# A two-layer hybrid decoder trunk: VectorE sums the opening's squares, one norm product, norm means in PSUM, and a new order of the attention steps

## The reference

```python
for l in range(DEPTH):                                  # 2
    h = rmsnorm(x, attn_norm[l])
    proj = einsum('bsd,de->bse', h, w_in[l])            # 1024 -> 2304 columns
    sb_q, sb_k, sb_v, sw_q, sw_k, sw_v = split(proj)    # 3 x 8 heads; 8, 2 and 2 heads, of 64
    sb_o = stick_breaking_attention(sb_q, sb_k, sb_v)   # strictly causal, in blocks of 128 queries:
        # z = q k / 8;  a = exp(log_sigmoid(z) + suffix sum of -softplus(z));  o = a v
    sw_q, sw_k = rope(sw_q, positions), rope(sw_k, positions)
    sw_o = sliding_window_sink_attention(sw_q, sw_k, sw_v, sinks[l])     # window 128, softmax with a sink
    mix = concat(rmsnorm(sb_o, sb_norm[l]), rmsnorm(sw_o, swa_norm[l]))
    x = x + einsum('bse,ed->bsd', mix, w_out[l])
    h = rmsnorm(x, mlp_norm[l])
    x = x + einsum('bsf,fd->bsd', square(relu(einsum('bsd,df->bsf', h, w_up[l]))), w_down[l])
return rmsnorm(x, final_norm)
```

## Time and profile before

| | us |
|---|---|
| median of 3 executions | 1188.58 (1187.75 to 1190.56) |
| the profiled execution | 1187.64 |
| its span, first to last instruction | 1185.9 |
| TensorE busy | 1154.5 (97%) |
| VectorE busy | 554.3 (47%) |
| ScalarE busy | 589.4 (50%) |
| GpSimd busy | 574.3 (48%) |

### The profile page before, as it was taken

The page is one execution under the profiler, slowest core; times in us unless marked ns, Lnnn a source line. Parts: engine busy times, 40 slices in busy tenths (PEclk is TensorE's granted clock), DMA queues, the critical chain, the costliest instruction groups (busy, mean ns, idle before and its releaser), DMA issues.

```text
span 1185.9 us, 15498 instructions
## 1 busy us (share of the span) xinstructions
PE 1154.5 (97%) x5546; PEld 968.4 (82%) x5546; DVE 554.3 (47%) x785; ACT 589.4 (50%) x940; POOL 574.3 (48%) x310
## 2 busy tenths in 40 slices
PE   7999998999999999999999999899999999999996
PEld 5788887878888888888888889687888888888886
DVE  7766678765222222223355666758532222222224
ACT  5789898544133233133346888965431422322442
POOL 3454754664444444444754564456454444444452
PEclk9999999999999999999999999999999999999999
DMA  5220211223322323222222121012233232232222
GB/s 188 72 71 19 90 36 36 91 87 99 99 94 100 107 88 105 90 89 96 99 72 72 54 69 50 25 54 90 89 107 107 89 103 93 88 106 88 97 81 72
DMA packets 30027, 99.65 MB, mean 84 GB/s; under 512 B 3600, under 2 KB 5648, under 8 KB 29968
## 3 DMA queue, kind: packets, MB, share of 16 engines
q1 hardware_dynamic: 28992, 97.80, 25.1%
q10 hardware_dynamic: 976, 1.08, 0.3%
HBM read 96.77 MB, written 2.10 MB: 83 GB/s over the span
## 4 chain that ended last, share of the span: by engine, by line
PE 88%; ACT 4%; DVE 3%; issue 1%; DVEq 1%; ACTq 1%; DMA 1%; SPq 0%
PE DW L441 24%; PE DW L443 24%; PE DW L442 24%; PE Z L441 2%; PE Z L443 2%; PE Z L442 2%; PE Z L594 2%; PE DW L528 2%; PE O L607 1%; PE Z L577 1%; PE O L552 1%; PE DW L524 1%; ACTq L813 1%; DMA raw<-in_weights 1%; PE DW L538 1%
## 5 line engine op out<-in xcount | busy, mean ns | idle before, releaser
L951 POOL TENSOR_TENSOR w<-raw,w 128x1024 fp32r<-128x1024 f32 x178 | 429.8, 2416 | 409.4 <-ACT w L701 405.5
L701 ACT ACTIVATE w<-raw 128x1024 fp32r<-128x1024 f32 x177 | 185.8, 1051 | 224.0 <-PE DW L443 212.4
L441 PE MATMUL DW<-xm,w 128*128 128x512 f32 x512 | 200.3, 391 | 1.6 <-issue 1.6
L441 PE MATMUL DW<-stage,w 128*128 128x512 f32 x512 | 199.5, 390 | 0.6 <-DVE stage L1256 0.6
L442 PE MATMUL DW<-xm,w 128*128 128x512 f32 x512 | 199.3, 389 | 0.0
L443 PE MATMUL DW<-xm,w 128*128 128x512 f32 x512 | 199.3, 389 | 0.0
L443 PE MATMUL DW<-stage,w 128*128 128x512 f32 x512 | 199.3, 389 | 0.0
L442 PE MATMUL DW<-stage,w 128*128 128x512 f32 x512 | 199.3, 389 | 0.0
L1281 DVE TENSOR_TENSOR kf<-o 128x512 f32<-128x512 f32 x64 | 58.1, 908 | 195.7 <-ACT o L886 195.5
L1297 DVE TENSOR_TENSOR DW<-DW,probs 128x512 f32<-128x512 f32 x62 | 43.4, 699 | 224.1 <-PE DW L443 224.1
L441 PE MATMUL DW<-xa,w 128*128 128x512 f32 x296 | 119.6, 404 | 9.5 <-DVE xa L1064 7.5
...
## 6 DMA issues: line engine op xcount, KB each, us to landing
raw<-in_weights SPq DMA_DIRECT2D x179, 512.0 KB, 3.3
...
```

Of the source, the lines that this page charges most:

```text
L441: pe.matmul(bank, w[:, slot, 0, k], rhs[:, 0, c], start=start, stop=False)
L701: act.activation(w[:, slot_of(l * PACKS + p), 0], raw[:, p % 2], ACT.Identity).then_inc(w_hi, 1)
L951: pool.tensor_tensor(w[:, slot, 1], raw[:, p % 2], w[:, slot, 0].bitcast(F32), ALU.subtract).then_inc(w_ready, 1)
```

## The change

- In the opening VectorE adds all eight squares by seven adds, in a tree, and splits the third pack between them; both had been in part GpSimd's. It begins the angle after that. GpSimd waits for the sum before its first split. `NP` is gone, and `NA` in layer 0 is one product of the whole sum.
- The mean of the attention, stick-breaking and MLP norms goes to the PSUM bank W in place of SBUF, and the first two refining steps too; the bank is freed after the last. The sliding-window norm and the closing ones stay as they were.
- The last head's BD: ScalarE squares into the bank O, and VectorE adds that.
- `zl_full` counts the last head's scores apart from the other heads'.
- Both lists of steps are ordered anew; the tiles are the same.

```diff
-T0 U0 AG0 T1 CH3 U1 NP0 NA0 NAE0 NAD0 NAF0 TE0 T2 CL3 AG1 TH0 CH4 AG2 CL4 AG3 T3 U2 U3 AG4 AG5 TL0 CH5 TE2 AG6
-RE2 TE1 AG7 AG8 T4 AG9 CL5 TH1 AG10 AG11 TL1 SN0 U4 TE3 RS2 RM2 RA2 RE3 RS3 RM3 TH2 T5 U5 TL2 RA3 CH6 TE4 TH3
...
-T8 XE1 XH0 XL0 XH1 U8 BE2 WE1 WR1 CH10 WN1 CH11 T9 XL1 BP2 BS3 TE8 BH2 WT1 U9 TH8 SQ0 WH1 BL2 BX2 SA0 TL8 WL1
...
-BP10 WA6 XH9 WT7 WO6 WD6 TH16 BS11 T17 WH7 WL7 BE11 SQ5 TL16 SA4 WA7 BP11 XL9 CL19 BH10 CH20 SQ6 WO7 SA5 BL10
-WD7 U17 BH11 BL11 BX10 SQ7 GH0 XE10 BA4 TE17 GL0 SA6 SA7 NW0 XH10 BO4 BS12 NWE0 BD4 NWD0 NWF0 BE12 MN0 BX11
-MN1 XL10 XE11 BS13 BP12 XH11 BE13 MN2 BP13 BH12 XL11 MH0 VT17 BL12 BH13 VH17 BA5 MN3 MH1 MH2 ML0 ML1 BL13 BX12
-GH1 MH3 VL17 BS14 BX13 XE12 XH12 ML2 XE13 BS15 BE14 BO5 ML3 BP14 XL12 BE15 XH13 OS0 CL20 BD5 OS1 BP15 BH14
-BH15 XL13 GH2 GL1 CH21 BL14 OS2 OS3 BA6 OE0 BX14 BL15 CH22 OE1 XE14 OE2 GL2 BX15 XE15 XH14 CL21 BO6 CL22 OE3
-CH23 OS4 OE4 XH15 BD6 XL14 OS5 XL15 OE5 CH24 BA7 OS6 CL23 BO7 BD7 CL24 OS7 GH3 OE6 OE7 GL3 NS0 NSE0 NSD0 NSF0
+T0 U0 T1 CH3 U1 NA0 NAE0 NAD0 NAF0 AG0 TE0 CL3 T2 T3 CH4 TH0 AG1 CL4 AG2 AG3 TE1 AG4 TL0 U2 U3 AG5 AG6 AG7 TE2
+AG8 AG9 T4 CH5 CH6 TH1 AG10 AG11 TL1 RE2 TE3 CL5 SN0 U4 RM2 RS2 T5 U5 RE3 RA2 TH2 RM3 RS3 TL2 RA3 TE4 TH3 CH7
+TL3 VT4 VH4 TE5 RE5 VL4 CL6 BS0 BS1 RM5 RS5 BE0 RA5 CL7 TH5 T6 TL5 CH8 BP0 CL8 U6 BH0 WS0 TE6 T7 VT6 WM0 WE0
+CH9 WR0 U7 BE1 BL0 VH6 BP1 TE7 WN0 BX0 TH7 VL6 WT0 WH0 CH10 XE0 WL0 TL7 T8 BH1 BS2 XH0 WS1 CL9 U8 BL1 WM1 CH11
...
+WN7 VL15 WA6 SA5 BE11 XH9 WT7 CL19 T17 U17 BL10 TH16 XL8 WO6 BP11 WH7 TL16 WD6 WL7 BH11 WA7 CH20 TE17 GH0 SQ6
+WO7 BX10 WD7 BL11 XL9 VT17 GH1 SQ7 VH17 VL17 BA4 XE10 GL0 SA6 XH10 SA7 BO4 NW0 BS12 NWE0 BD4 XL10 NWD0 NWF0
+BE12 BX11 MN0 XE11 XH11 BS13 MH0 XL11 BP12 MN1 MN2 BE13 BH12 BS14 BP13 MH1 BL12 MH2 BH13 MN3 BS15 ML0 BA5 BE14
+ML1 BL13 BX12 MH3 XE12 ML2 XH12 ML3 BX13 BP14 BO5 OS0 XL12 OE0 BH14 XE13 OS1 OS2 BE15 OS3 CH21 CL20 XH13 BD5
+CL21 XL13 BA6 BL14 CH22 BP15 BH15 BL15 GH2 CH23 BX14 BO6 GL1 XE14 OE1 BX15 OS4 XH14 BD6 XE15 XH15 OS5 GL2 XL14
+OE2 OE3 XL15 BA7 BO7 CL22 OE4 OS6 BD7 GH3 OS7 CL23 OE5 NS0 GL3 CH24 NSE0 OE6 NSD0 NSF0 OE7 CL24
...
-T0 T1 CH3 U0 CH4 NA0 U1 CL3 NAE0 CL4 NAD0 NAF0 TE1 RE1 T2 TE0 TH0 TL0 U2 RS1 TE2 RE2 T3 RM1 RM2 RA1 CH5 CL5
-TH1 U3 TL1 TE3 T4 RS2 RA2 RE3 RM3 RS3 CH6 TH2 RA3 TL2 U4 TH3 CL6 TE4 T5 TL3 VT4 WS0 WM0 U5 CH7 VH4 WE0 VL4 TE5
-T6 WR0 WN0 TH5 TL5 U6 WT0 BS0 WH0 WL0 BS1 TE6 CL7 WS1 CH8 BE0 CL8 VT6 CH9 BP0 T7 VH6 VL6 BH0 WM1 U7 BE1 CH10
-BL0 CL9 BX0 WA0 WE1 TE7 T8 WR1 WO0 WN1 XE0 BP1 BH1 XH0 TH7 BL1 WT1 WH1 WL1 BX1 BS2 XE1 CH11 BS3 WS2 CL10 U8
...
-TL17 BX10 NW0 XE10 BS12 NWE0 BE12 NWD0 NWF0 BA4 MN0 BX11 MN1 XH10 BO4 XE11 MN2 BS13 BP12 BS14 MN3 MH0 BH12
-BE13 CL20 BL12 ML0 BS15 BX12 GL0 XH11 XL10 BP13 MH1 MH2 BD4 XL11 BH13 BL13 BA5 ML1 MH3 ML2 ML3 BE14 BP14 XE12
-BX13 XE13 BH14 XH12 OS0 BO5 OS1 BL14 OE0 XL12 BE15 BD5 BX14 BP15 XH13 XL13 OS2 GH1 BH15 XE14 BA6 BL15 CH21
...
+CH3 T0 CL3 T1 NA0 T2 NAE0 U0 NAD0 CH4 NAF0 U1 TE1 CH5 TE0 RE1 U2 TH0 RS1 CL4 TL0 T3 U3 RM1 RA1 TH1 TL1 TE2 RE2
+TE3 T4 RS2 CL5 RE3 CH6 RM2 RM3 RA2 CH7 RS3 TH2 RA3 T5 TH3 TL2 U4 TL3 CL6 WS0 TE4 CH8 VT4 VH4 WM0 WE0 VL4 U5 T6
+TE5 CL7 WR0 WN0 TH5 TL5 U6 WT0 CH9 WH0 BS0 WL0 BS1 TE6 WS1 BE0 BP0 VT6 BE1 WM1 VH6 BH0 BP1 CL8 T7 WE1 BL0 CH10
+WR1 U7 VL6 WN1 BX0 WA0 TE7 TH7 TL7 WT1 BH1 BL1 T8 WH1 CL9 WL1 WO0 XE0 BX1 BS2 WS2 XH0 WD0 XE1 BE2 CH11 WM2 BP2
...
+TE16 BP11 SA5 U17 SQ6 VT16 XL9 BX10 WO7 BH11 WD7 TE17 CH20 SQ7 SA6 BL11 GH0 VH16 SA7 VL16 TH17 NW0 XE10 TL17
+BS12 NWE0 NWD0 NWF0 MN0 MN1 BA4 MN2 BE12 XH10 BX11 BP12 XE11 BS13 MH0 BO4 BH12 ML0 BE13 CL20 BL12 XH11 GH1 MH1
+XL10 GL0 MN3 BP13 BD4 BH13 BS14 MH2 BS15 MH3 BL13 ML1 BE14 BX12 XL11 ML2 BA5 ML3 BP14 BO5 BX13 XE12 XE13 BH14
+XH12 OS0 BD5 OS1 BE15 OS2 BL14 BP15 GH2 OE0 OS3 BH15 XL12 BL15 BX14 OE1 CH21 CH22 CL21 GL1 XH13 OE2 XE14 BX15
...
-                    elif step == "NP":
-                        pe.wait_ge(masks, 5)
-                        pe.wait_ge(w_drained, 1)
-                        pe.wait_ge(start_added, 1)
-                        add_norm(sq_start[0], True, False)
-                        pe.wait_ge(start_summed, 1)
-                        add_norm(sq_start[2], False, False)
                     elif step == "NA":
                         if l == 0:
-                            pe.wait_ge(start_summed, 2)
-                            add_norm(sq_start[4], False, True).then_inc(w_full, 1)
+                            pe.wait_ge(masks, 5)
+                            pe.wait_ge(w_drained, 1)
+                            pe.wait_ge(start_summed, 1)
+                            add_norm(sq_start[0], True, True).then_inc(w_full, 1)
...
-                        mm.then_inc(z_full, 1)
+                        mm.then_inc(zl_full if h == LAST_HEAD else z_full, 1)
...
-                        act.wait_ge(z_full, l * PIECES + n + 1)
+                        if h == LAST_HEAD:
+                            act.wait_ge(zl_full, l * 2 + n % 2 + 1)
+                        else:
+                            act.wait_ge(z_full, l * Z_PIECES + n + 1)
...
+                    elif step == "BD" and n == LAST_HEAD:
+
+                        act.wait_ge(o_joined, l + 1)
+                        act.activation(O[:, :], o[:, n // 2 % 2], ACT.Square).then_inc(o_squared, 1)
...
-            pool.wait_ge(sq_full, 2)
-            pool.wait_ge(w_ready, 2)
-            pool.tensor_tensor(sq_start[0], sq_start[0], sq_start[1], ALU.add).then_inc(start_added, 1)
-            split(0, 2)
             pool.memset(group_rows[:, :], 0.0)
             pool.drain()
             for a in range(4):
                 pool.memset(group_rows[a * DH // 2:(a + 1) * DH // 2, a % 2:a % 2 + 1], 1.0)
             pool.drain()
+            pool.wait_ge(start_summed, 1)
...
-                dve.tensor_scalar(mean, sums, -1.0 / width, EPS, ALU.mult, ALU.add).then_inc(w_drained, 1)
-
-            def norm_refine(count, mean, guess, dst):
+                return dve.tensor_scalar(mean, sums, -1.0 / width, EPS, ALU.mult, ALU.add)
+
+            def norm_refine(count, mean, guess, dst, last=None):
...
-                dve.scalar_tensor_tensor(dst, dst, 1.5, guess, ALU.add, ALU.mult)
-                dve.drain()
+                dve.scalar_tensor_tensor(dst if last is None else last, dst, 1.5, guess, ALU.add, ALU.mult)
+
+            def refine_in_psum(count, dst):
+
+                norm_refine(count, W[:, 0, :], work1, W[:, 0, :], dst)
+                dve.drain().then_inc(w_drained, 1)
...
+            def sum_squares(a, b):
+
+                dve.wait_ge(sq_full, b + 1)
+                return dve.tensor_tensor(sq_start[a], sq_start[a], sq_start[b], ALU.add)
+
+            sum_squares(0, 1)
+            sum_squares(2, 3)
+            first_split(2)
+            dve.drain()
+            sum_squares(0, 2)
+            sum_squares(4, 5)
+            sum_squares(6, 7)
+            dve.drain()
+            sum_squares(0, 4)
+            dve.drain()
+            sum_squares(0, 6)
+            dve.drain().then_inc(start_summed, 1)
             dve.wait_ge(positions_loaded, 32)
...
-            dve.wait_ge(sq_full, 4)
-            dve.tensor_tensor(sq_start[2], sq_start[2], sq_start[3], ALU.add).then_inc(start_summed, 1)
-            for c in (4, 6):
-                dve.wait_ge(sq_full, c + 2)
-                dve.tensor_tensor(sq_start[c], sq_start[c], sq_start[c + 1], ALU.add)
-            dve.drain()
-            dve.tensor_tensor(sq_start[4], sq_start[4], sq_start[6], ALU.add).then_inc(start_summed, 1)
...
-                        norm_mean(l * len(NORMS) + NORMS["attention"], DM, work0)
+                        norm_mean(l * len(NORMS) + NORMS["attention"], DM, W[:, 0, :])
                     elif step == "NAF":
-                        norm_refine(l * len(NORMS) + NORMS["attention"], work0, work1, rms_a[:, :])
+                        refine_in_psum(l * len(NORMS) + NORMS["attention"], rms_a[:, :])
...
-                        if n % 2:
+                        if n == LAST_HEAD:
+                            dve.drain().then_inc(o_joined, 1)
+                            dve.wait_ge(o_squared, l + 1)
+                            dve.tensor_tensor(acc[:, 1], acc[:, 1], O[:, :], ALU.add)
+                            dve.drain().then_inc(sb_o, 1)
+                        elif n % 2:
```

More of the change, by code:

```diff
@@ L100 @@
 PIECES = 2 * SB_HEADS
+Z_PIECES = PIECES - 2
 ORDER_0 = """
-T0 U0 AG0 T1 CH3 U1 NP0 NA0 NAE0 NAD0 NAF0 TE0 T2 CL3 AG1 TH0 CH4 AG2 CL4 AG3 T3 U2 U3 AG4 AG5 TL0 CH5 TE2 AG6
-RE2 TE1 AG7 AG8 T4 AG9 CL5 TH1 AG10 AG11 TL1 SN0 U4 TE3 RS2 RM2 RA2 RE3 RS3 RM3 TH2 T5 U5 TL2 RA3 CH6 TE4 TH3
-VT4 CH7 TL3 CL6 VH4 TE5 BS0 BS1 RE5 VL4 RM5 BE0 T6 RS5 RA5 TH5 TL5 BE1 U6 TE6 BP0 WS0 VT6 CL7 BH0 WM0 WE0 CH8
-T7 BP1 BH1 U7 VH6 BL0 WR0 WN0 BL1 WT0 BX0 WH0 CL8 TE7 WL0 TH7 XE0 CH9 VL6 BX1 CL9 WA0 WO0 WS1 BS2 WD0 WM1 TL7
@@ L153 @@
-CL19 WE7 BE10 TE15 VT15 BD3 WR7 XE9 XH9 WN7 SA4 U16 SQ5 SA5 BP10 WA6 VH15 VL15 WT7 XL8 WO6 XL9 BS11 BH10 WD6
```

(4 more changed lines are left out.)

69 lines of the change are left out of this document (36 added, 33 removed).

## The result

| | before | after |
|---|---|---|
| median of 20 executions each, one chip | 1189.01 us (1187.75 to 1191.62) | 1191.04 us (1190.44 to 1192.46) |
| ratio, 95% interval | | 1.0016 (1.001 to 1.0022) |
| profiled execution, its span | 1187.64, 1185.9 | 1190.56, 1188.8 |

The kernel became slower by 2 us, and I had said 1.6 us faster. The interval excludes no change; 1191.04 is above the range's upper end of 1190.0.

A forecast was written before the change was run, and what follows sets the result against it. It took TensorE, busy 1154.5 of 1185.9 us, as the bound. Opening -1.0, middle -1.0, layer 0's tail +0.5, layer 1's -0.1 made -1.6 us: 1186.0 profiled, 1187.0 median; 8-in-10 range 1184.0 to 1190.0.

The forecast's parts named there:

- The opening, -1.0: Start of layer 0: two norm products fewer save 1.94 us of TensorE, of which 1.0 us comes through at T5.
- The cover of 0.6 us: Opening: the sum of squares is ready at 20.5, TensorE arrives at 21.09, so the norm product doesn't wait.
- Ended when that did: Opening: VectorE's 2.88 us add at 19.34 was read as ending together with GpSimd's split of 18.96 to 21.67.
- I take 14.4 - 0.5 = 13.9: Opening: VectorE's time from TE0 to TL1's drain, less 0.49 us idle, so TL1 is drained 1.0 us earlier.
- The middle, -1.0: Both layers' middles: the new order gains somewhat less than half of TensorE's 2.7 us idle; ends -2.7 and +1 us.
- 4 us together: Whole kernel: the total taken for all TensorE waits outside the four listed entries.
- The tail of layer 0, +0.5: End of layer 0's attention: BE14 ahead of MH3 releases OS0 at 193.1 against 192.79; ends -1 and +3.9 us.
- rival C: Slower: ScalarE enters layer 0's tail late, OS0 up to 3.9 us later; 1190.4 to 1191.7 us; chance 0.15.
- in my walk XE10 isn't late: Layer 0's tail: XE10 isn't late because BX10 itself waits behind U17 and WA7 fills the time.
- The tail of layer 1, -0.1: End of layer 1's attention: OS0's release comes out at nearly the old place; ends -1 and +1.3 us.
- Norms in PSUM and the hand-over, 0: Norm means and refining steps in PSUM cost 0; the last head's squares on ScalarE 0, at worst 0.7 us per layer.
- B: Rival: nothing arrives, TensorE's gains before the tails are waited away at BS12, BS13 and OS0; 1188.6 us; chance 0.18.

The follow-up runs named there:

- sums alone: The kernel before with its old lists and only VectorE's seven adds, the third pack's split and one norm product: 1188.44 us, 0.9997 of before.
- both-old-lists: The changed kernel with both layers' old lists of steps (NP0 left out): 1188.58 us, 1.0001 of the kernel before.
- the middle alone: The changed code with both old lists, but layer 0's middle, first window scores to BX10, after the new list: 1190.47 us, 1.0012 of before.
- the unused matmuls: The changed code with both old lists, plus 10 (layer 0) and 6 (layer 1) matmuls computing nothing used, ahead of BS13: 1187.65 us, 0.9992 of before.

## Why the prediction was wrong

**The opening, -1.0.** TensorE's part was right to 0.3 us in the profiled execution: 1.9 us saved, no wait before the norm product, sum ready at 20.6 (I had 20.5). The cover of 0.6 us was luck, though: in seven of 15 traces the norm product waited up to 0.93 us. "Ended when that did" was a wrong reading of the add at 19.34: it ended at 22.22, 0.55 us behind GpSimd's split. Mis-sized was the step behind it, "I take 14.4 - 0.5 = 13.9" from TE0 to TL1's drain. The idle half microsecond that I took out stands again, 0.55 at 35.22, and TE0 came at 27.88 in place of 27.6, so TL1's row starts 0.26 us earlier than before and not 1.0. T4 waits 2.05 us (1.4 forecast), T5 1.68 at full clock. Of 1.9 us, 0.3 arrive at WS0, and that is less than WS0 moves between traces of the old opening order under the changed code (55.73 to 56.50). Nothing of it can be told in the time: sums alone and both-old-lists are at 0.9997 and 1.0001, with 1 us of uncertainty. A lead of 2.1 us was lost in one execution, with 10.24 us at half clock, and kept (2.5 us at the MLP's start) where TensorE didn't idle; over all executions it reached the time. That the tail eats the opening's gain is so not shown; mostly it didn't reach the first scores.

**The middle, -1.0.** This is the step that failed, in sign. I took "somewhat less than half" of TensorE's idle time as the gain because idle time was there to be won. The new order of layer 0 makes more small gaps than it closes, +1.7 us in the changed kernel's trace and +1.6 in that of the middle alone, and layer 1's gives +0.4 in the trace. I had bounded the two middles together at 1 us more. What I walked, layer 1's BX1, came out: its wait of 0.9 is gone. WT1 exceeds the pitch by 0.31 there, where I had 0.6. A place of that kind and size, 0.58 for GpSimd, stands at layer 0's WT2, and its cause can be read. On TensorE WA1, about 1 us, stood between WS2 and WT2 and now stands ahead of WS2: WS2 ends 1.1 us later and WT2 has that much less cover. On VectorE TL8 and BP3 come 3 to 4 us later than in both-old-lists, so WM2's reduction (L1246) starts 0.6 us behind WS2 and not 0.2:

```profile
88.25 1.22 DVE L1246 TENSOR_REDUCE small<-DW 128x4 f32<-128x1024 f32 x1
```

```profile
86.65 1.23 DVE L1246 TENSOR_REDUCE small<-DW 128x4 f32<-128x1024 f32 x1 [1.47 <-PE DW L524]
```

(the first the changed kernel, the second both-old-lists). L1255, which releases GpSimd's probabilities, comes at 92.52 in place of 90.69. The causes at BS8 and BA3, and of the 0.9 us in small joints, stay open. I walked one place of one layer closely and took a share for the other 120 us. I also had the waits outside the four entries at "4 us together", where the list of before has 7.6.

**The tail of layer 0, +0.5.** Right in direction, and the size is partly luck: +0.84 against before and +0.41 against both-old-lists. BE14's stretch was right: it stands ahead of MH3, and OS0 waits 0.75 us for ML3, 10.33 us behind XE11 (I had said about 10), only 0.12 more than the 10.21 of before. The other 0.72 is made ahead of XE11, where I had 0.1: XE10 is late behind BX10 by 1.0 us, which is what rival C had said and I had denied in "in my walk XE10 isn't late". NW0's wait of 0.35 came out where I had 0.4; BX13's of 0.71 wasn't forecast.

**The tail of layer 1, -0.1.** 0.0: BX10 and OS0 are both 2.4 us later than before.

**Norms in PSUM and the hand-over, 0.** Right as far as the intervals tell. The row decides against the dearer PSUM source that I weighed from the Trainium skill ("VectorE: DVE Perf Modes", the section on the TRN2 errata): 0.70 us with PSUM in and out, 0.69 in SBUF.

**The rivals.** B had nothing arrive because the tail waits it away; nothing arrived, but for the most part it wasn't there at the first scores. C gave the right time (1190.4 to 1191.7) by a mechanism that carries only a third: it put 3.9 us into the tail and had 2.1 gained ahead of it; measured are 0.8 in the tail, and a loss ahead of it.

**What the forecast left out** is that the time of before isn't one number. Its 20 executions beside the changed kernel go from 1187.75 to 1191.62, and in the 35 beside the unused matmuls the time goes with the granted clock. In the traces the half clock that moves the end of layer 0's attention is the one behind BS13's wait. The changed kernel's 20 go from 1190.44 to 1192.46, and its seven at a mean clock of 0.993 average 0.5 us more than its three at 0.998: its tail waits for the other engines anyway. In medians that makes 2.0 us, from the lowest times 2.7 (1190.44 against 1187.75).
